# Expert outputs of a PEER layer: token parts interleaved by element, weight slabs stored backwards and read with a negative step

## What is computed

```python
q = (xb @ w_pq).reshape(PEER_BLOCK, P_HEADS, 2, P_HALF)
sc = jnp.einsum('thpc,hpkc->thpk', q, sub_keys)
...
g = jax.nn.softmax(fv.astype(jnp.float32), axis=-1).astype(xb.dtype)
ue = jnp.take(u_experts, eid, axis=0)
ve = jnp.take(v_experts, eid, axis=0)
a = jax.nn.gelu(jnp.einsum('thkd,td->thk', ue, xb), approximate=False)
return jnp.einsum('thk,thkd->td', g * a, ve)
```

## Time and profile before

| what | value |
|---|---|
| median of 3 runs | 2074.11 us (2073.15 to 2077.49) |
| the profiled execution's own time | 2075.4 us |
| its span, first to last instruction | 2073.7 us |
| granted TensorE clock, mean | 0.998 |
| busy: PE, PEld, DVE, ACT, POOL | 2047.3, 1756.5, 1652.6, 1191.7, 343.5 us |
| V stages, layer 1 and layer 2 | 682 to 1035 us and 1717 to 2052 us |
| matmuls | 11544, of which 3072 on lines 1698 and 1720 |

### The profile page before, as it was taken

One profiled execution on the slowest core, in us unless ns is written; L12 is line 12 of the kernel. 1 busy time (PEld: TensorE's weight loads), 2 busy tenths in 40 slices (PEclk: granted clock), 3 DMA queues, 4 the chain that ended last, 5 costly groups with the idle time before them and its releaser, 6 DMA issues.

```text
span 2073.7 us, 38360 instructions
## 1 busy us (share of the span) xinstructions
PE 2047.3 (99%) x11544; PEld 1756.5 (85%) x11544; DVE 1652.6 (80%) x3041; ACT 1191.7 (57%) x1901; POOL 343.5 (17%) x342
## 2 busy tenths in 40 slices
PE   8999999999999999999999999999999999999998
PEld 6888888888888888888878888888888897888886
DVE  7786769999998677777788858799999986766666
ACT  6555556666666555555565545666766665555553
POOL 4010110000000333333340102000000003333331
PEclk9999999999999999999999999999999999999999
DMA  6445457776656877777653554577756568777773
GB/s 226 142 162 172 165 194 238 235 233 206 200 192 204 279 241 241 241 240 242 211 184 126 188 173 164 199 235 239 222 197 198 196 205 280 243 241 241 242 240 127
DMA packets 174249, 435.54 MB, mean 210 GB/s; under 512 B 19504, under 2 KB 85040, under 8 KB 173136
## 3 DMA queue, kind: packets, MB, share of 16 engines
q1 hardware_dynamic: 173520, 430.06, 63.4%
q0 software_dynamic: 640, 4.32, 0.6%
HBM read 397.60 MB, written 36.70 MB: 209 GB/s over the span
## 4 chain that ended last, share of the span: by engine, by line
PE 90%; DVE 5%; ACT 2%; DMA 2%; issue 1%; SPq 0%; POOL 0%; ACTq 0%; DVEq 0%
PE ps L1698 32%; PE ps L1317 31%; PE ps L1318 16%; PE ps L1673 3%; PE ps L1589 2%; DVE w_lo L835 2%; PE ps L1311 2%; DMA h_park<-h_out 1%; DMA raw<-slabs 1%; PE ps L1720 1%; ACT w_hi L712 1%; PE ps L1614 1%; PE ps L1648 1%; PE ps L1571 1%; DVE pick L1173 0%
## 5 line engine op out<-in xcount | busy, mean ns | idle before, releaser
L835 DVE TENSOR_TENSOR w_lo<-raw,w_hi 128x1024 fp32r<-128x1024 f32 x674 | 840.2, 1247 | 264.7 <-ACT w_hi L780 191.6
L1317 PE MATMUL ps<-act,w_hi 128*128 128x512 f32 x2784 | 986.2, 397 | 0.0
L1318 PE MATMUL ps<-act,w_lo 128*128 128x256 f32 x2784 | 777.2, 279 | 0.0
L1317 PEld LDWEIGHTS ps<-act,w_hi 128*128 128x128 f32 x2784 | 522.4, 188 | 117.4 <-issue 3.0
L1698 PE MATMUL ps<-w_hi,act 128*128 128x512 f32 x1936 | 596.5, 389 | 2.6 <-DVE act L1238 2.6
L1318 PEld LDWEIGHTS ps<-act,w_lo 128*128 128x128 f32 x2784 | 525.8, 189 | 0.1
L780 ACT ACTIVATE w_hi<-raw 128x1024 fp32r<-128x1024 f32 x248 | 263.1, 1061 | 325.0 <-PE ps L1698 313.3
L1698 PEld LDWEIGHTS ps<-w_hi,act 128*128 128x128 f32 x1936 | 363.5, 188 | 78.5 <-DVE act L1238 3.4
L1698 PE MATMUL ps<-w_lo,act 128*128 128x512 f32 x968 | 376.6, 389 | 0.0
L511 POOL TENSOR_TENSOR h_in<-h_in,gate 128x256 f32<-128x256 f32 x250 | 241.9, 968 | 444.3 <-DMA h_in<-h_park 444.1
L712 ACT ACTIVATE w_hi<-raw 128x1024 fp32r<-128x1024 f32 x248 | 261.1, 1053 | 0.0
(11 more groups left out here) (261 smaller groups left out, 1826.0 us busy)
## 6 DMA issues: line engine op xcount, KB each, us to landing
raw<-slabs SPq DMA_DIRECT2D x680, 512.0 KB, 4.2
h_park<-h_out SPq DMA_DIRECT2D x256, 128.0 KB, 2.1
h_in<-h_park SPq DMA_DIRECT2D x250, 128.0 KB, 3.9
memT<-mem POOLq DMA_DIRECT2D x2, 1024.0 KB, 5.6
skT<-sub_keys POOLq DMA_DIRECT2D x2, 1024.0 KB, 7.2
x_park<-xT SPq DMA_DIRECT2D x2, 1024.0 KB, 6.4
xT<-x_park SPq DMA_DIRECT2D x2, 1024.0 KB, 8.2
xT<-x SPq DMA_DIRECT2D x4, 256.0 KB, 5.5
```

Source lines behind the costliest of these rows:

```text
L835: nc.vector.tensor_tensor(w_lo[:, j].rearrange("p k c -> p (k c)"), raw[:, j, :], w_hi[:, j].rearrange("p k c -> p (k c)").bitcast(FP32), ...
L1317: nc.tensor.matmul(ps[:, j, :], w_hi[:, j, k, :], a[:, :, k, :], start=(k == 0), stop=False)
L1318: return nc.tensor.matmul(ps[:, j, hi * T:hi * T + T], w_lo[:, j, k, :], a[:, hi, k, :], start=False, stop=(k == KB - 1))
```

## The change

In the V stage alone:

1. The gated activations' parts lie interleaved by element in one tile, act_v[partition, slot, token block, token, part]: a high part's next element is its neighbour two elements (8 bytes) on, between them lie the low parts. ScalarE writes the high, VectorE the low ones with that step, and TensorE loads its stationary operand with it. The tile starts 64 bytes (PHASE) past a multiple of 1024.
2. ScalarE writes w_hi backwards (element 1023 first), VectorE reads w_hi and writes w_lo backwards, raw is read forwards. TensorE reads the 512 columns backwards, from the other half of the slab, so that PSUM gets its columns in the order it had.
3. h_in and y_nat move behind act_v; the tiles behind them move by 512 bytes.

The first three slabs' token parts stay as they were, contiguous; their weights too are written and read backwards. No instruction, wait or transfer is added, removed or moved on any queue.

```diff
+PHASE = 64
...
-        y_nat = [at(f"y_nat{b}", act_at + (2 * b + 1) * RING * T * 4, [P, 2, 512]) for b in range(TB)]
-        h_in = at("h_in", act_at + RING * T * 4, [P, RING, T])
+        act_v = at("act_v", act_at + PHASE, [P, RING, TB, P, 2], F32R)
+        h_at = act_at + 2 * RING * T * 4 + 512
+        top[0] += 512
+        y_nat = [at(f"y_nat{b}", h_at + b * RING * T * 4, [P, 2, 512]) for b in range(TB)]
+        h_in = at("h_in", h_at, [P, RING, T])
...
-                    nc.scalar.activation(w_hi[:, j].rearrange("p k c -> p (k c)"), raw[:, j, :],
+                    nc.scalar.activation(w_hi[:, j].rearrange("p k c -> p (k c)")[:, ::-1], raw[:, j, :],
                                          ACT.Copy).then_inc(hi_ready, 1)
...
-                    nc.scalar.activation(hi[:, j:j + 1, :], h[:, j:j + 1, :], ACT.Copy).then_inc(ga_hi_ready, 1)
+                    nc.scalar.activation(act_v[:, j, :, :, 0], h_in[:, j, :].rearrange("p (b t) -> p b t", b=TB),
+                                         ACT.Copy).then_inc(ga_hi_ready, 1)
...
+            def expert_lo(layer, at0, g, j):
+
+                dve.wait_ge(hi_ready, layer * SLABS + at0 + g * RING + j + 1)
+                nc.vector.tensor_tensor(w_lo[:, j].rearrange("p k c -> p (k c)")[:, ::-1], raw[:, j, :],
+                                        w_hi[:, j].rearrange("p k c -> p (k c)")[:, ::-1].bitcast(FP32),
+                                        ALU.subtract).then_inc(lo_ready[j], 1)
...
-                    nc.vector.tensor_tensor(lo[:, j:j + 1, :], h[:, j:j + 1, :], hi[:, j:j + 1, :].bitcast(FP32),
-                                            ALU.subtract).then_inc(ga_ready, 1)
+                    nc.vector.tensor_tensor(act_v[:, j, :, :, 1], h_in[:, j, :].rearrange("p (b t) -> p b t", b=TB),
+                                            act_v[:, j, :, :, 0].bitcast(FP32), ALU.subtract).then_inc(ga_ready, 1)
...
-                    lo_part(layer, V_AT, 0, j)
+                    expert_lo(layer, V_AT, 0, j)
...
-                        lo_part(layer, V_AT + RING, g, j)
+                        expert_lo(layer, V_AT + RING, g, j)
...
+                def tokens(j, b, part):
+                    return act_v[:, j, b, :, part]
...
-                            for i, (w, a) in enumerate(((w_hi, hi), (w_lo, hi), (w_hi, lo))):
-                                last = nc.tensor.matmul(ps[:, 2 * b + half, :], a[:, j, b * P:(b + 1) * P],
-                                                        w[:, j, 4 * half:4 * half + 4, :].rearrange("p k c -> p (k c)"),
+                            for i, (w, part) in enumerate(((w_hi, 0), (w_lo, 0), (w_hi, 1))):
+                                last = nc.tensor.matmul(ps[:, 2 * b + half, :], of(j, b, part),
+                                                        w[:, j, 4 - 4 * half:8 - 4 * half, :].rearrange("p k c -> p (k c)")[:, ::-1],
                                                         start=(first and i == 0), stop=(final and i == 2))
```

More of the change, by code:

```diff
@@ L763, in _, with gated_hi, early_gated_hi @@
                 assert n == GROUPS
-                def gated_hi(g, j, hi=act_hi, h=h_in):
+                def gated_hi(g, j):
                     act.wait_ge(gated_ready, layer * V_SLABS + g * RING + j + 1)
-                    nc.scalar.activation(hi[:, j:j + 1, :], h[:, j:j + 1, :], ACT.Copy).then_inc(ga_hi_ready, 1)
+                    nc.scalar.activation(act_v[:, j, :, :, 0], h_in[:, j, :].rearrange("p (b t) -> p b t", b=TB),
+                                         ACT.Copy).then_inc(ga_hi_ready, 1)
+                def early_gated_hi(j):
+                    act.wait_ge(gated_ready, layer * V_SLABS + j + 1)
+                    nc.scalar.activation(early_hi[:, j:j + 1, :], early_in[:, j:j + 1, :], ACT.Copy).then_inc(ga_hi_ready, 1)
                 for j in range(RING):
@@ L772, in _ @@
                     if j < EARLY:
-                        gated_hi(0, j, early_hi, early_in)
+                        early_gated_hi(j)
                     else:
@@ L1234, in _, with gated_lo, early_gated_lo @@
                     lo_part(layer, U_AT + TAIL_AT, 0, j)
-                def gated_lo(g, j, hi=act_hi, lo=act_lo, h=h_in):
+                def gated_lo(g, j):
                     dve.wait_ge(ga_hi_ready, layer * V_SLABS + g * RING + j + 1)
-                    nc.vector.tensor_tensor(lo[:, j:j + 1, :], h[:, j:j + 1, :], hi[:, j:j + 1, :].bitcast(FP32),
-                                            ALU.subtract).then_inc(ga_ready, 1)
+                    nc.vector.tensor_tensor(act_v[:, j, :, :, 1], h_in[:, j, :].rearrange("p (b t) -> p b t", b=TB),
+                                            act_v[:, j, :, :, 0].bitcast(FP32), ALU.subtract).then_inc(ga_ready, 1)
+                def early_gated_lo(j):
+                    dve.wait_ge(ga_hi_ready, layer * V_SLABS + j + 1)
+                    nc.vector.tensor_tensor(early_lo[:, j:j + 1, :], early_in[:, j:j + 1, :],
+                                            early_hi[:, j:j + 1, :].bitcast(FP32), ALU.subtract).then_inc(ga_ready, 1)
                 for j in range(RING):
-                    lo_part(layer, V_AT, 0, j)
+                    expert_lo(layer, V_AT, 0, j)
                     if j < EARLY:
-                        gated_lo(0, j, early_hi, early_lo, early_in)
+                        early_gated_lo(j)
                     else:
@@ L1687, in _, with early_tokens, expert_out @@
                 group(layer, U_AT + TAIL_AT, U_EV + TAIL_AT)
-                def expert_out(g, j, first=False, final=False, hi=act_hi, lo=act_lo):
+                def tokens(j, b, part):
+                    return act_v[:, j, b, :, part]
+                def early_tokens(j, b, part):
+                    return (early_hi, early_lo)[part][:, j, b * P:(b + 1) * P]
+                def expert_out(g, j, first=False, final=False, of=tokens):
                     pe.wait_ge(lo_ready[j], lo_count(layer, V_AT, g))
@@ L1705, in _ @@
                 for j in range(EARLY):
-                    expert_out(0, j, first=(j == 0), hi=early_hi, lo=early_lo)
+                    expert_out(0, j, first=(j == 0), of=early_tokens)
                 expert_out(0, EARLY)
@@ L1718, in _ @@
                         for b in range(TB):
-                            for i, (w, a) in enumerate(((w_hi, act_hi), (w_lo, act_hi), (w_hi, act_lo))):
-                                last = nc.tensor.matmul(ps[:, 2 * b + half, :], a[:, j, b * P:(b + 1) * P],
-                                                        w[:, j, 4 * half:4 * half + 4, :].rearrange("p k c -> p (k c)"),
+                            for i, (w, part) in enumerate(((w_hi, 0), (w_lo, 0), (w_hi, 1))):
+                                last = nc.tensor.matmul(ps[:, 2 * b + half, :], tokens(j, b, part),
+                                                        w[:, j, 4 - 4 * half:8 - 4 * half, :].rearrange("p k c -> p (k c)")[:, ::-1],
                                                         start=False, stop=(j == RING - 1 and i == 2))
```

## The result

The changed kernel takes 2092.26 us (median of 3 runs, 2091.98 to 2096.46) against 2074.11: 1.0093 times as long, 95% interval 1.007 to 1.0116. The forecast was 2043 us, faster; it is slower by 18 us.

The account below looks back on a forecast made before the run. TensorE was taken as the bound, busy 99% of the span. 10.4 ns x 3000 matmuls = 31.2 us off 2075.4 gave 2044.2, and the run median 1.3 lower 2043 us; range 2038 to 2080.

Parts of the forecast that it names:

- I take 2.9: V-stage matmuls: time beyond the columns' own falls from 13.3 to 2.9 ns, as in gate matmuls; 31.2 us gained.
- the remainder: V-stage matmuls: 13.3 ns of each 226.7 ns pitch beyond 213.3 for 512 columns; at most 41 us to gain.
- only turn the moving read; I give them nothing: First three slabs of each layer, 72 matmuls with contiguous tokens: turned weights alone were to change nothing, 0 us.
- it falls when the stationary load is short: Time beyond the columns' own: 8.1 ns beside an 8-column load against 13.3, read as two reads obstructing each other.
- The interleaved load gets in the way more: Rival: V-stage load touches twice the length, 24.1 ns beyond the columns; 32.4 us lost, 2106 us; chance 0.09.
- A backward read is slow: Rival: backward operands run slower, 2700 us if on TensorE, 2222 us if on VectorE; chance 0.10.
- No change: Rival: the 13.3 ns is a fixed price of V-stage matmuls whatever the addresses; 2074 us; chance 0.18.
- rule of independent ports: Counter-argument: TensorE's two operands have independent SBUF read ports, so the layout could not move the pitch; gain nought.
- charge for each crossing to a new line: Cited for the worse-load rival: each crossing to a new 16-byte line is charged, and interleaving doubles the crossings.

Follow-up runs that it names:

- contiguous_backward: Kernel before with only its V-stage weights stored and read backwards, token parts contiguous and unmoved; 2093.19 us, 233.3 ns a matmul.
- forward_shift64: Kernel before with its contiguous token parts moved 64 bytes further on, weights forwards; 2092.23 us, 233.3 ns a matmul.
- forward_load8: Kernel before with two stationary loads in three cut from 128 to 8 columns, weights forwards; 233.3 ns a matmul in one layer, 227.0 in the other.
- backward_load64: Kernel before with weights backwards and two stationary loads in three cut to 64 columns; 233.3 ns a matmul.
- both_places: Changed kernel (interleaved tokens, backward weights) with each slot's two token blocks at places of their own instead of 64 bytes for all; 2094.62 us.
- interleaved_forward: Changed kernel without the turning: weights forwards, interleaved tokens and 64-byte shift kept; 2086.86 us, 1.0064 times the kernel before.

## Why the prediction was wrong

**Right:** that nothing but the pitch of the V stage's matmuls would move the time, that VectorE and ScalarE would write backwards at their old pace, that their stepped writes (32 ns longer on ScalarE, where none was forecast) and all transfers would stay hidden, and that lines 1317 and 1318 would keep theirs. The sum of the loss has the form that was forecast, a difference per matmul times 3072; its sign was wrong.

**The step that failed** is the term "I take 2.9": the remainder beside 512 columns was to fall from 13.3 to 2.9 ns, 10.4 gained a matmul, and it rose to 20.0, 6.7 lost. Two things under it were wrong. The first is the turned read, put at nothing: "only turn the moving read; I give them nothing". By itself it costs 6.7 ns a matmul, for those 72 and for all others (contiguous_backward, 233.3 ns). The second is where the cure came from, four remainders of unlike matmuls, and above all "it falls when the stationary load is short": the 8.1 ns beside a load of 8 columns came from line 1442, with 256 moving columns and other operands. When loads of 8 columns were put beside two in three of the V stage's own matmuls, the pitch was 226.7 or 233.3, with no saving by length. The 2.9 of the gate matmuls belongs to another type and another width. None of the distances, steps and directions tried brought the remainder at 512 columns under 13.3. Whether the two reads do get in each other's way is neither shown nor refuted: the place of the stationary operand moves the pitch, its length doesn't shorten it.

**The rivals.** "The interleaved load gets in the way more" had the right sign and came nearest in time (2106 us, decided "as soon as the remainder passes 13.3"), but by luck, not by the cause: at one and the same shift interleaving lowered the pitch, from 233.3 to 230.0. "A backward read is slow" had the right operand; its price on TensorE was not the 204 ns of a read at half pace but 6.7 at 512 columns, and on VectorE nothing. I had bounded it by the pace of plain fp32, which is far off, and so saw it as a disaster or nothing. A backward read that costs half of the remainder again was in no case. "No change" rested on the remainder being a fixed price whatever the addresses: forward_shift64 refutes that.

**What was cited.** By the Trainium skill's rule of independent ports ("TensorE: Matmul & The Clock Gate", Step-by-step), as the prediction read it, the layout would have left the pitch where it was; it did move it, and the measurement decides. As far as the length of the load goes, forward_load8 and backward_load64 agree with the rule. The Trainium skill's charge for each crossing to a new line ("SBUF — State Buffer", DMA port swizzle, note on cachelines) may be in the 6 ns by which an interleaved load's record is longer; in the pitch it doesn't show, since interleaving, which doubles the crossings, lowered it at the same shift.

**Shown:** the turned read alone is enough for all of the loss (contiguous_backward, 233.3 ns), and beside it the tokens' step, place and load length change next to nothing, one slot of both_places apart. Without it the changed layout would still lose half, 3.3 ns (interleaved_forward). **Open:** why a 512-column backward read settles at 233.3 ns and a forward one at 226.7, 230 or 233.3 by the place of the stationary operand and, it may be, the way the stream began. A collision in the memory and a rhythm inside TensorE would both do; a stationary operand loaded in the other direction, which would help to tell them apart, wasn't tried.

## What to carry to other kernels

A few ns left over beside each matmul add up where there are thousands, but remainders of other types, widths and shapes don't say what they are made of: put the suspected cause beside the very matmul that is to gain, here a short load, before a layout is built on it. A layout with three changes wants three kernels with one each: the shift and the turning, each alone, would have shown the loss. Where a stream is at its best, a move of an operand by 64 bytes, such as a new tile ahead of it makes, can cost a percent without one instruction being different.

## What was not expected of the hardware

The pitch of 512-column fp32r matmuls came out, as a mean over a V stage, at 226.7, 230.0 or 233.3 ns wherever operands stayed in one place, 3.3 ns apart, and nowhere between except in kernels that changed places or load lengths as they went. Two of these paces appeared for the same instructions on the same addresses in the two layers of one execution (forward_load8: 347.19 and 337.82 us for 1488 matmuls). And a backward read, slower at 512 columns (233.3 against 226.7 ns), is quicker at 256 (118.4 against 120.0).
